# Filler matmuls ahead of lone products in a chunked recurrence, two-block layer on one core

## The chip, the cores and the metric

One core of one Trainium2 chip runs the whole program. The metric is the device time of one execution in microseconds (us); the kernel before has a median of 2063.27 us over 3 runs (2058.55 to 2068.33).

## The reference, cut to what matters

The reference is a stack of two blocks on 512 tokens of width 1024: an RWKV-7 mixer with two attention groups and an output projection, and then a sparse-attention layer, an HGRN2 layer and two gated feed-forward layers. The change lies in the RWKV-7 part alone. It computes, for 8 heads of 64 by 64 state,

```
def step(S, inp):
    r_t, w_t, k_t, v_t, kk_t, a_t = inp
    sa = jnp.einsum('bhvk,bhk->bhv', S, -kk_t)
    S = (S * w_t[:, :, None, :]
         + sa[..., None] * (kk_t * a_t)[:, :, None, :]
         + v_t[..., None] * k_t[:, :, None, :])
    y = jnp.einsum('bhvk,bhk->bhv', S, r_t)
    return S, y
```

over 512 steps. The inputs of the recurrence are prepared elementwise (a decay, a rate `a`, a key normed per head), and a per-head term `sum(r * k * r_k) * v` is added to its output.

## The kernel before, in words

The program is a row of stages, each a block with one instruction stream for each engine, and a barrier of all engines between two stages (`end_stage`, line 87). Weights flow in slabs of 512 KB through a ring of four. Three stages matter here.

**stage_rwkv_prep** (line 494) prepares the recurrence. TensorE makes four head sums of squares (L548), eight products of the two low-rank projections (L555), and, when VectorE has worked through a tile `m` of four (L582 to L591, semaphore `rk_out`), one head sum of `r * k * r_k` into bank `m` (L559). VectorE multiplies the four sums with v at its very end (L595). The order of the work on each engine is that of the code.

**stage_rwkv_chunks** (line 613) computes the recurrence in eight chunks of 64 steps (`NCH` is 8, `CH` is 64). The order is written out by `rwkv_steps` (line 598): ten turns, each with five levels, and at each level the names in `first` belong to chunk `s`, those in `rest` to chunk `s - 1` and those in `state` to chunk `s - 2`. So turn 0 holds the first part of chunk 0 alone, turn 1 the first part of chunk 1 and the `rest` of chunk 0, turns 2 to 7 all three kinds, turn 8 the `rest` of chunk 7 and the `state` of chunk 6, and turn 9 the `state` of chunk 7. TensorE walks this list (the loop `for key in steps`): it waits until the bank of the product is free (`before`), then for the operands (`need`), then issues the product. Products `ga` and `gb` are L701, `ma` and `mb` L706, `vt` L713, `bt` L716, `et` L746, both parts of `uy` L768 and L773, `y` L782, `st` L787 and `yt` L792; all others (`p1`, `p1t`, `p2`, `p2t`, `r2`, `p3t`, `r3`, `r4`, `x`, `xt`, `x2t`, `v1`, `w`, `sa`) go through the helper `each`, eight 64 by 64 matmuls at L688. Six banks go round for all of these but `uy` and `y`, which have banks 6 and 7. ScalarE and VectorE copy or add the results out of the banks in the same order (L806 to L815; L846 to L893), and `p1` also waits for three GpSimd operations (L828, L829, L831), which start when `gb` is out of its bank.

**stage_middle** (line 1024) follows. It loads eight small tables by DMA, and TensorE starts with L1062, L1064 and L1067.

The helper `warm` (line 161) is in the kernel already: it issues `n` matmuls of the identity with 256 columns of constants into a bank that the next product overwrites (L164). Before the change the two attention stages use it.

```
def warm(c, pe, bank, n):
    for _ in range(n):
        pe.matmul(bank[:, 0:2 * P], con(c, "ident"), c.cst[:, 0:2, :], start=True, stop=True)
```

Of the kernel before, what the change touches and what calls it, by code (L numbers as in the profile page):

```python
# [160 lines left out]
# [4 lines that stand above are left out]
# [97 lines left out]
def con(c, name):  # L262
    return c.cst[:, CB[name], :]


def wk(c, at, *shape):

    n = int(np.prod(shape))
    v = c.work[:, at:at + n]
    if len(shape) == 1:  # L270
        return v
    names = "abcd"[:len(shape)]
    return v.rearrange(f"p ({' '.join(names)}) -> p {' '.join(names)}", **dict(zip(names[1:], shape[1:])))
# [205 lines left out]
NCH = T // CH  # L479
# [14 lines left out]
def stage_rwkv_prep(c):  # L494
# [11 lines left out]
    with nc.Block() as block:  # L506

        @block.sync
        def _(sp):
            sp.dma_start(c.reset[:, :], c.a["reset"]).then_inc(reset_in, 16)  # L510
# [33 lines left out]
        @block.tensor  # L544
        def _(pe):
            for m in range(4):
                pe.wait_ge(sq_out, m + 1)
                pe.matmul(c.bank[4 + m][:, :], con(c, "blk"), c.h[:, m, :], start=True, stop=True).then_inc(norm_made, 1)  # L548
            pe.wait_ge(tanh, 1)
            for m in range(4):  # L550
                for j in range(2):
                    if m >= 2:
                        pe.wait_ge(up_out, 2 * (m - 2) + j + 1)
                    rows = slice(HD * j, HD * j + HD)
                    pe.matmul(c.bank[2 * (m % 2) + j][:, :], c.wup[rows, m * P:(m + 1) * P], wa[rows, 0, :],  # L555
                              start=True, stop=True).then_inc(up_made, 1)
            for m in range(4):
                pe.wait_ge(rk_out, m + 1)
                pe.matmul(c.bank[m][:, :], con(c, "blk"), iclr[:, m, :], start=True, stop=True).then_inc(rk_made, 1)  # L559

        @block.vector
        def _(dve):
# [50 lines left out]
def stage_rwkv_chunks(c):  # L613
# [6 lines left out]
    w = [c.h[:, 6 + i, :] for i in range(2)]  # L620
# [7 lines left out]
    yt = wk(c, 8192, 4, T)  # L628
# [3 lines left out]

    by_dve = ("ga", "gb", "ma", "mb", "r2", "r3", "r4", "xt", "v1", "w", "sa", "st", "yt")
    made_at = {key: i + 1 for i, key in enumerate(steps)}
    out_at, turn, before, held = {}, {}, {}, {}
    counts = {"dve": 0, "act": 0}
    for key in steps:
# [16 lines left out]
    def bank(key):  # L654
        return c.bank[turn[key]]

    def need(eng, *key):

        e, n = out_at[key]
        eng.wait_ge(dve_out if e == "dve" else act_out, n)  # L660
# [17 lines left out]
    with nc.Block() as block:  # L678
# [6 lines left out]
        def _(pe):  # L685
# [5 lines left out]
            for key in steps:  # L691
                name, ch = key
                b = buf[ch % 2]
                if before.get(key):
                    need(pe, *before[key])
                if name in ("ga", "gb"):
                    for h in range(4):

# [1633 lines left out]
def program(nc, aps, out):  # L2332

    with ExitStack() as ctx:
        c = Ctx(nc, ctx, aps)
        alloc(c)
        stages = (
            lambda: stage_in(c),
            lambda: stage_rwkv_prep(c),
            lambda: stage_rwkv_chunks(c),  # L2340
            lambda: stage_middle(c),
            lambda: stage_nsa(c),
            lambda: stage_project(c, "out", PLAN["out"], 1.0, ("rms", ("final_g", 0), None, 0), dsa_parts),
            lambda: stage_dsa_in(c),
            lambda: stage_dsa(c),
            lambda: stage_project(c, "wo", PLAN["wo"], ALPHA, ("ln", ("ln_g", 0), ("ln_b2", 0)), ffn_parts),
            lambda: stage_ffn(c, 0),
            lambda: stage_hgrn(c),
            lambda: stage_project(c, "ho", PLAN["ho"], ALPHA, ("ln", ("ln_g", 2 * KT), ("ln_b2", 2 * KT)), ffn_parts, c.big[:, 8:16, :]),
            lambda: stage_ffn(c, 1),  # L2350
            lambda: stage_store(c, out),
        )
        for stage in stages:
            stage()
            c.end_stage()
# [148 lines left out]
```

## Time and profile before

| what | value |
|---|---|
| median of 3 runs | 2063.27 us (2058.55 to 2068.33) |
| the profiled execution, its own time | 2068.71 us |
| its span, first to last instruction | 2066.5 us |
| mean granted TensorE clock | 0.927 |
| TensorE busy | 1865.5 us, 90% of the span |
| VectorE busy | 935.9 us, 45% |
| ScalarE busy | 840.5 us, 41% |
| GpSimd busy | 251.9 us, 12% |
| filler matmuls (L164) before | 324 records for 162 matmuls |
| chunk stage, first product to the next stage's | 260.77 to 428.76 us |

Durations below are of the one profiled execution, with times counted from its span's start. An f32 matmul leaves two records in the trace. PEclk is the TensorE clock that was granted in a stretch, as a share of full speed: 0.50 is 1.2 GHz, 1.00 is 2.4 GHz, and a value between them is a stretch that had some of both. In a timeline row the first number is the start, the second the time covered, xN the number of records, and the bracket the idle time of the engine before it with what ended it; matmuls overlap one another, so a row's cover is longer than the time until the next product can be issued.

### The profile page before, as it was taken

To read this page: it belongs to the slowest core of one execution; us is meant where nothing else is said; L and a number is where in the kernel's file an instruction comes from. 1 tells how busy PE (TensorE), PEld (TensorE's weight loads), DVE (VectorE), ACT (ScalarE), POOL (GpSimd) and SP (SyncE) were. 2 spreads that over 40 slices of the span, in tenths; PEclk is the share of its full clock that TensorE was granted. 3 is DMA by queue.
4 is the path that set the end of the run, shared out by engine and by line. 5 is a ranking of instruction groups with operands and counts; after the bars stand their busy time and mean duration, and the time that the engine had idled before them with its cause. 6 is when DMAs were issued, how large, how long until landed. Compare 5 with 4: busy or idle time off the path is not lost. (4 is left out here: it accounts for less than half of the span.)

```text
span 2066.5 us, 31549 instructions
## 1 busy us (share of the span) xinstructions
PE 1865.5 (90%) x12592; PEld 1512.1 (73%) x12592; DVE 935.9 (45%) x1622; ACT 840.5 (41%) x1359; POOL 251.9 (12%) x209
## 2 busy tenths in 40 slices
PE   5999389969978889988999999979999879999996
PEld 4888188857756657666788888868887768888885
DVE  2343935463355677745333333265554443333333
ACT  4322334434533443543443432275654343434222
POOL 3000223220003220002100000032221020000000
PEclk9999559869989989998999999999999879999998
DMA  4321010010012100002223233222221213233331
GB/s 167 99 92 56 0 43 3 3 45 1 1 42 69 59 23 1 1 27 76 82 91 101 92 101 92 92 79 71 71 78 37 72 51 98 95 98 95 99 95 51
DMA packets 37762, 131.69 MB, mean 64 GB/s; under 512 B 4816, under 2 KB 5136, under 8 KB 37392
## 3 DMA queue, kind: packets, MB, share of 16 engines
q1 hardware_dynamic: 36784, 127.91, 19.8%
q8 instruction: 83, 1.36, 0.3%
q10 hardware_dynamic: 864, 2.17, 0.3%
q14 instruction: 31, 0.25, 0.0%
HBM read 127.17 MB, written 2.10 MB: 63 GB/s over the span
## 5 line engine op out<-in xcount | busy, mean ns | idle before, releaser
L138 DVE TENSOR_TENSOR big_parts<-ring,big_parts 128x1024 fp32r<-128x1024 f32 x164 | 205.0, 1252 | 526.3 <-ACT big_parts L133 526.3
L156 PE MATMUL bank<-h_parts,big_parts 128*128 128x512 f32 x960 | 381.3, 397 | 26.3 <-POOL y_parts L1406 17.6
L157 PE MATMUL bank<-y_parts,big_parts 128*128 128x512 f32 x960 | 377.7, 393 | 0.0
L158 PE MATMUL bank<-h_parts,big_parts 128*128 128x512 f32 x960 | 377.1, 393 | 0.0
L133 ACT ACTIVATE big_parts<-ring 128x1024 fp32r<-128x1024 f32 x164 | 173.7, 1061 | 287.6 <-PE bank L158 287.4
L156 PEld LDWEIGHTS bank<-h_parts,big_parts 128*128 128x128 f32 x960 | 182.8, 190 | 67.5 <-issue 28.6
L158 PEld LDWEIGHTS bank<-h_parts,big_parts 128*128 128x128 f32 x960 | 182.7, 190 | 38.5
L157 PEld LDWEIGHTS bank<-y_parts,big_parts 128*128 128x128 f32 x960 | 182.7, 190 | 37.0
L157 PE MATMUL bank<-y_parts,work_parts 128*128 128x512 f32 x456 | 181.4, 398 | 0.0
L138 DVE TENSOR_TENSOR work_parts<-ring,work_parts 128x1024 fp32r<-128x1024 f32 x65 | 79.3, 1222 | 167.7 <-ACT work_parts L133 167.7
L133 ACT ACTIVATE work_parts<-ring 128x1024 fp32r<-128x1024 f32 x65 | 68.7, 1060 | 206.0 <-PE bank L158 175.9
L156 PE MATMUL bank<-big_parts 128*128 128x512 f32 x352 | 136.9, 389 | 0.0
L157 PE MATMUL bank<-work_parts,big_parts 128*128 128x512 f32 x352 | 136.9, 389 | 0.0
L158 PE MATMUL bank<-big_parts 128*128 128x512 f32 x352 | 136.9, 389 | 0.0
L156 PE MATMUL bank<-h_parts,work_parts 128*128 128x512 f32 x232 | 94.8, 409 | 23.6 <-DVE work_parts L138 19.8
L973 ACT ACTIVATE work<-work 128x256 f32<-128x256 f32 (+4 forms) x128 | 67.1, 524 | 112.7 <-DVE work L995 112.5
L156 PE MATMUL bank<-work_parts 128*128 128x512 f32 (+1 forms) x256 | 97.7, 382 | 5.7 <-POOL y_parts L180 3.8
L157 PEld LDWEIGHTS bank<-y_parts,work_parts 128*128 128x128 f32 x456 | 88.2, 193 | 18.6 <-issue 0.2
L158 PE MATMUL bank<-work_parts 128*128 128x512 f32 (+1 forms) x256 | 97.0, 379 | 0.0
L164 PE MATMUL bank<-cst 128*128 128x256 f32 x324 | 96.5, 401 | 0.0
L158 PE MATMUL bank<-h_parts,work_parts 128*128 128x512 f32 x232 | 92.9, 401 | 0.0
L995 DVE CUSTOM_DVE_ANT_0 work<-bank,big 128x256 f32<-128x256 f32 (+3 forms) x112 | 53.9, 481 | 83.0 <-PE bank L944 72.4
(402 smaller groups left out, 3020.3 us busy)
## 6 DMA issues: line engine op xcount, KB each, us to landing
ring<-in_wstream SPq DMA_DIRECT2D x229, 512.0 KB, 3.5
x<-in_xt SPq DMA_DIRECT2D x4, 512.0 KB, 7.7
out_t<-x SPq DMA_DIRECT2D x8, 256.0 KB, 2.0
work<-in_memt ACTq DMA_DIRECT2D x1, 1024.0 KB, 14.6
work<-in_cw SPq DMA_DIRECT2D x1, 1024.0 KB, 5.1
cst<-in_cst ACTq DMA_DIRECT2D x1, 704.0 KB, 7.7
cos<-in_reset SPq DMA_DIRECT2D x2, 256.0 KB, 2.7
big<-work SPq DMA_DIRECT2D x4, 128.0 KB, 4.2
```

Of the source, the lines that this page charges most:

```text
L133: act.activation(self.parts[:, self.place_of(n), 0, :, :], self.ring[:, n % RING, :, :], ACT.Copy).then_inc(self.slab_cast, 1)
L138: dve.tensor_tensor(self.parts[:, self.place_of(n), 1, :, :], self.ring[:, n % RING, :, :], self.parts[:, self.place_of(n), 0, :, :].bitca ...
L156: pe.matmul(out, w[0], x[0], start=start, stop=False, skip_group_check=True)
L157: pe.matmul(out, w[0], x[1], start=False, stop=False, skip_group_check=True)
L158: return pe.matmul(out, w[1], x[0], start=False, stop=stop, skip_group_check=True)
L164: pe.matmul(bank[:, 0:2 * P], con(c, "ident"), c.cst[:, 0:2, :], start=True, stop=True)
L973: act.activation(e, e, ACT.Exp, bias=self.low[:, n:n + 1], scale=-1.0, accum_out=self.den[:, n:n + 1])\
L995: dve.tensor_tensor_reduce(self.weights(n), self.c.bank[self.SCORES[n % 3]][:, 0:u.keys], u.mask, -self.scale, 3e38, ALU.add, ALU.min, sel ...
```

## The change

It issues fillers at two places. In the preparation stage six go ahead of the wait for each of the four head sums, and three behind the last. In the chunk stage two go ahead of each product named in the set `lone`: nine products of chunk 0 and seven of chunk 7, behind the wait for the bank and ahead of the wait for the operands. With 27 and 32 that makes 59 filler matmuls. Nothing is removed.

```diff
@@ stage_rwkv_prep, tensor
             for m in range(4):
+                warm(c, pe, c.bank[6], 6)
                 pe.wait_ge(rk_out, m + 1)
                 pe.matmul(c.bank[m][:, :], con(c, "blk"), iclr[:, m, :], start=True, stop=True).then_inc(rk_made, 1)
+            warm(c, pe, c.bank[6], 3)
@@ stage_rwkv_chunks
     made_at = {key: i + 1 for i, key in enumerate(steps)}
+    lone = {(n, 0) for n in ("p1", "p2", "p3t", "r4", "et", "x", "x2t", "v1", "w")}
+    lone |= {(n, NCH - 1) for n in ("et", "x", "x2t", "v1", "w", "sa", "yt")}
     out_at, turn, before, held = {}, {}, {}, {}
@@ stage_rwkv_chunks, tensor
                 if before.get(key):
                     need(pe, *before[key])
+                if key in lone:
+                    warm(c, pe, bank(key), 2)
                 if name in ("ga", "gb"):
```

The set is a table, so here is what it does to TensorE's order. The first place is turn 0 of the chunk stage, from the last two transposes to `r4` of chunk 0. Before (L688 rows are `p1`, `p1t`, `p2` and `p2t`):

```order
L713 MATMUL bank4<-cst,big 128x128 x4
L716 MATMUL bank5<-cst,work 128x128 x4
L688 MATMUL bank0<-big 64x64 x8
L688 MATMUL bank1<-big 64x64 x8
L688 MATMUL bank2<-big 64x64 x8
L688 MATMUL bank3<-big 64x64 x8
```

and now (L692 is the same helper, moved down by the new lines; the rows from bank 5 on are `p3t`, `r3` and `r4`):

```order
L719 MATMUL bank4<-cst,big 128x128 x4
L722 MATMUL bank5<-cst,work 128x128 x4
L164 MATMUL bank0<-cst 128x256 x2
L692 MATMUL bank0<-big 64x64 x8
L692 MATMUL bank1<-big 64x64 x8
L164 MATMUL bank2<-cst 128x256 x2
L692 MATMUL bank2<-big 64x64 x8
L692 MATMUL bank3<-big 64x64 x8
L692 MATMUL bank4<-big 64x64 x8
L164 MATMUL bank5<-cst 128x256 x2
L692 MATMUL bank5<-big 64x64 x8
```

Two fillers stand ahead of the first product of each level, in its own bank; the other products of the level follow without any. The second place is the end of the stage: `w` of chunk 7, then `uy`, `sa`, `y` and `yt` of chunk 7. Before:

```order
L688 MATMUL bank0<-big,y 64x64 x8
L768 MATMUL bank7<-work,h 64x64 x16
L773 MATMUL bank7<-work 128x128 x4
L688 MATMUL bank1<-work,h 64x64 x8
L782 MATMUL bank7<-work,h 64x64 x8
L792 MATMUL bank2<-cst,work 128x64 x4
```

and now:

```order
L164 MATMUL bank0<-cst 128x256 x2
L692 MATMUL bank0<-big,y 64x64 x8
L774 MATMUL bank7<-work,h 64x64 x16
L779 MATMUL bank7<-work 128x128 x4
L164 MATMUL bank1<-cst 128x256 x2
L692 MATMUL bank1<-work,h 64x64 x8
L788 MATMUL bank7<-work,h 64x64 x8
L164 MATMUL bank2<-cst 128x256 x2
L798 MATMUL bank2<-cst,work 128x64 x4
```

`uy` and `y`, which are not in the set, get none.

## Rows read from the trace of the kernel before

**Rows 1.** The page: granted clock in 40 slices of the span, in tenths.
```profile
PEclk9999559869989989998999999999999879999998
```
**Rows 2.** Stretches: turns 0, 1, 2 with 3, 4, and turns 8 with 9.
```profile
260.77:277.61 16.84, 12.55 (x184) 11.63 (x186) 3.72 (x8) 4.98 (x12) 3.70 (x3) 0.60 0.34 126
277.61:296.71 19.10, 18.08 (x285) 17.31 (x284) 6.84 (x16) 7.26 (x18) 3.71 (x3) 0.50 0.01 2
296.71:332.15 35.44, 33.98 (x726) 32.06 (x725) 18.20 (x41) 16.66 (x40) 12.11 (x14) 0.85 0.01 3
332.15:349.11 16.96, 15.14 (x371) 14.20 (x368) 9.46 (x22) 8.32 (x20) 6.04 (x7) 1.00 0.01 2
402.57:428.76 26.19, 21.61 (x257) 19.61 (x257) 7.09 (x16) 4.68 (x11) 0.04 (x1) 0.51 0.01 2
```
**Rows 3.** Timeline and stretches: the twelve fillers that open the attention stage.
```profile
469.62 7.94 PE L164 MATMUL bank<-cst 128*128 128x256 f32 x24
477.39 0.27 PE L953 MATMUL bank<-cst,work 128*31 128x128 f32 x1
...
470.00:475.00 5.00, 5.00 (x13) 3.98 (x13) 0.43 (x6) 0.68 (x4) 0.00 (x0) 0.53 0.00 0
475.00:480.00 5.00, 5.00 (x32) 3.81 (x31) 0.71 (x6) 1.43 (x7) 0.00 (x0) 1.00 0.00 0
```
**Rows 4.** Timeline: end of the preparation stage.
```profile
212.23 5.97 PE L555 MATMUL bank<-big,wup 64*128 64x512 f32 x16 [2.63 <-ACT big L520]
...
243.41 2.07 PE L559 MATMUL bank<-work,cst 128*128 128x512 f32 x2 [25.22 <-DVE work L591]
...
257.14 2.08 PE L559 MATMUL bank<-work,cst 128*128 128x512 f32 x2 [2.50 <-DVE work L591]
259.26 0.69 DVE L595 TENSOR_TENSOR y<-bank,big 128x512 f32<-128x512 f32 x1 [0.37 <-PE bank L559]
```
**Rows 5.** Timeline: turn 0 of the chunk stage.
```profile
264.48 1.26 POOL L828 TENSOR_TENSOR big<-h,cst 64x512 f32<-64x512 f32 x1 [23.13 <-DVE h L862]
...
268.28 1.15 PE L688 MATMUL bank<-big 64*64 64x64 f32 x32 [1.88 <-issue]
...
270.71 4.98 PE L688 MATMUL bank<-big 64*64 64x64 f32 x80 [1.28 <-ACT big L806]
271.87 1.62 ACT L806 ACTIVATE big<-bank 64x256 f32<-64x256 f32 x4 [1.30 <-PE bank L688]
...
275.73 0.86 DVE L851 TENSOR_TENSOR big<-bank,big 64x256 f32<-64x256 f32 x2 [1.30 <-PE bank L688]
276.74 1.12 PE L688 MATMUL bank<-big 64*64 64x64 f32 x16 [1.04 <-DVE big L851]
```
**Rows 6.** Timeline: products of turns 4 and 7, at full clock.
```profile
338.84 1.15 PE L688 MATMUL bank<-big 64*64 64x64 f32 x32 [1.18 <-issue]
339.79 0.66 PE L688 MATMUL bank<-big,work 64*64 64x64 f32 x16
...
384.88 1.24 PE L701 MATMUL bank<-work 64*64 64x128 f32 x26
386.84 0.66 PE L713 MATMUL bank<-cst,big 128*128 128x128 f32 x4
387.86 0.51 PE L746 MATMUL bank<-cst,big 64*64 64x64 f32 x10
389.23 1.16 PE L773 MATMUL bank<-work 128*128 128x128 f32 x8
395.92 1.09 PE L782 MATMUL bank<-work,h 64*64 64x64 f32 x16
396.94 1.16 PE L787 MATMUL bank<-work 128*128 128x128 f32 x8
```
**Rows 7.** Timeline: end of the chunk stage, start of the next.
```profile
402.57 0.51 PE L746 MATMUL bank<-cst,y 64*64 64x64 f32 x10 [0.54 <-DVE y L851]
...
427.57 0.43 DVE L893 COPY work<-bank 128x256 f32<-128x256 f32 x1 [3.49 <-PE bank L792]
...
437.08 2.87 DVE L1136 TENSOR_TENSOR work<-big,work 128x496 f32<-128x496 f32 x2 [1.44 <-DMA work<-in_cmask]
```

## The prediction

> **What bounds the kernel now.** I read the page's clock slices first [rows 1]. TensorE is busy for 90% of the span, so its clock is what matters, and the two slices at five tenths are the fifth and sixth of 51.7 us each, 207 to 310 us. That is the end of the preparation stage and turns 0 and 1 of the chunk stage.
>
> The stretches by turn [rows 2] say what this costs. Turn 1 takes 19.10 us at a clock of 0.50 and is busy for 18.08 of them, so it is bound by TensorE at half speed. Turn 4, with a third set of products on top, takes 16.96 at 1.00. Turn 0 takes 16.84 at 0.60, and turns 8 and 9 together 26.19 at 0.51. The reader should see two things: these are the stretches that the change touches, and having work to do did not bring the clock up: 19 us of nearly solid 64 by 64 products in turn 1 ran at half.
>
> Fillers are matmuls of 128 rows and 128 columns. The attention stage has twelve that start at half clock, and the clock goes up while nothing else runs on TensorE: 0.53 over 470 to 475, 1.00 from 475 [rows 3]. 0.53 over 5 us is 0.3 us at full, so it rose at about 474.7, 5.1 us after the first filler.
>
> **Price of a filler.** Those 24 records fill the 7.77 us until the next matmul [rows 3]. With 5.1 us at half and 2.67 at full, and a record at full taking half of one at half (an assumption from the two clock levels), (5.1 + 2 x 2.67) / 24 = 0.435 us a record at half. A filler is two records: 0.87 us at half, 0.435 at full. A pair is 1.74 or 0.87.
>
> **Preparation, 27 fillers.** The first six start when L555 is done, near 218.2, and are over by 221 at full, in a gap of 25.22 us [rows 4]; 22 us of idle time follow, so they bring nothing and cost nothing. The sum of tile 0 starts at 243.41 at half, and six fillers follow at once. A steady run of 128 by 128 work took 5.1 us to lift the clock [rows 3]; here that is by 248.5. Up to then 0.87 us x 6 = 5.2 us of fillers are partly at half, and tile 1, due 4.58 us after tile 0 ((257.14 - 243.41) / 3), starts about 1 us late. Nobody waits: VectorE reads the sums only at its end. From tile 2 on, 2.6 us of fillers fit in the 4.58. VectorE's last multiply starts 2.12 us after the last sum (259.26 against 257.14); at full I take 1.06, so it ends near 258.9 instead of 259.95. The three closing fillers end near 257.14 + 0.9 + 1.3 = 259.3 and now end the stage. Gain 0.5 us. Bounds: -2 if the clock is not up (sum and fillers then end near 257.14 + 1.7 + 2.6 = 261.5), +1.
>
> **Turn 0, 4 pairs.** The first product `p1` waits for GpSimd, whose chain is unchanged. In turn 4, at full clock, the product behind that wait starts 338.84 - 332.15 = 6.7 us after its turn did; in turn 0 it takes 268.28 - 260.77 = 7.5. With nothing of a previous chunk ahead of GpSimd I take 6.4, which gains 1.1. TensorE has issued its own work by then (3.0 us at full: 384.88 to 387.86 [rows 6]), and the pair ahead of `p1` falls in the wait: free. From `p1` on, a level is a product, its copy and the next product. `p2` follows `p1` by 2.43 at full (268.28 to 270.71, [rows 5], where the clock was up for the moment). `p3t` then waits for two copies: 0.7 until the first starts and 1.62 for both, 2.4 in all; `r3` is 0.47 later (two products take 0.95, 338.84 to 339.79 [rows 6]), its VectorE add ends 0.7 + 0.86 after that, and `r4` starts. That is 6.4 + 2.4 + 2.4 + 0.5 + 1.7 = 13.4, and the turn ends 0.5 later: 13.9 against 16.84. The three inner pairs (0.87 each) end before the operands are there: `p1` and `p1t` plus a pair is 1.8 against 2.4; `p2`, `p2t`, `r2` and a pair is 2.3 against 2.4; `p3t`, `r3` and a pair is 1.8 against 2.2. They are free as long as the clock is up; at half, 1.74 each, they would not be. Gain 3.0.
>
> **Turn 1, 5 pairs.** At full, TensorE's part is 3.0 for the products that open it, 14 products of the L688 kind at 0.47 (6.6), and 5 pairs (4.4); nothing hides the last four, since TensorE is the bound here. `p1` of chunk 1 cannot start before 6.4, and `et` with its pair is done at 4.4: 2.0 idle. Sum 16.0 against 19.10. Gain 3.1. Without fillers but at full it would be 12.5 (the wait until 6.4, then 13 products at 0.47), so the cure costs three of the six it could give.
>
> **Turns 2 and 3** get no fillers but may inherit the clock: 35.44 at 0.85 against two times 16.96 [rows 2]. Gain 1.5 at most.
>
> **Turns 8 and 9, 7 pairs.** At full, the products are: eight of the 0.47 kind, 3.8; `uy` twice (389.23 - 387.86 - 0.47 = 0.9 for the first part, 1.06 for the second, by `st`'s), 3.9; `y` twice at 1.02, 2.0; `st` 1.1; `yt` twice at 0.4, 0.8 [rows 6]. That is 11.6, and pairs 6.1: 17.7. On top 1.6 us of waits that remain: for the last `sa` copy (1.2) and short ones. So the last copy ends 19.3 after the first product, where it was 428.00 - 402.57 = 25.4 [rows 7]. Gain 6.1.
>
> **What does not follow.** The next stage starts sooner by the whole gain and with a clock that is up. But its VectorE chain waits for a DMA that is issued at the stage's start, until 437.08 [rows 7], and TensorE's head start ends there. I count nothing.
>
> Sum with the clock up throughout: 0.5 + 3.0 + 3.1 + 1.5 + 6.1 = 14.2 us.
>
> **Relapses.** The waits for GpSimd in turns 0 and 1 leave 2.6 and 2.0 us idle (6.4 less 3.0 and a pair; 6.4 less 4.4). In turn 0 before, the clock that was up at 268.28 was at half again for the products from 270.71 on, after idle gaps of 1.88 and 1.28 [rows 5], so it can fall there. A relapse puts `p1`, `p1t` and the next pair at half: 0.95 + 0.87 more, of which turn 0 has 0.6 to spare (2.4 - 1.8), and in turn 1 `x` and `xt` also (0.95): 1.2 to 2.8 us. I count one of 2.2. Forecast: 14.2 - 2.2 = 12.0.
>
> The Trainium skill ("TensorE: Matmul & The Clock Gate", Part 1) says that sustained TensorE activity opens the clock and idle time closes it, whatever the matmuls are. By that rule turn 1 before should have run at full; the trace disagrees (18.08 of 19.10 busy, 0.50). By the rule, turn 1 would have nothing to gain, and the sum would be 5.4 in place of 12.0; I go by the rows, and keep that outcome as the second rival.
>
> The profiled execution took 2068.71 us, 5.4 more than the median, so the sum reads 2056.7 on it and **2051.3 on the median**. A measurement here can tell about 0.5%, 10.3 us, from no change, so the forecast lies only just beyond that.
>
> **Rivals.**
> - *The clock relapses at each wait.* For it: the two gaps above. 14.2 less 1.2 and 2.8, and 2.2 for one more in turn 8, leaves 8: 2055.3. Chance 0.27.
> - *The other executions had less to win.* The median execution is 5.4 us faster than the profiled one, and part of that may be a turn 1 with its clock up. Then turn 1 loses 3.5 to its fillers (16.0 against 12.5) where I count a gain of 3.1: 12.0 - 6.6 = 5.4, or 2057.9. One trace of one execution can't exclude it. Chance 0.14. (By the skill's rule this would be the ordinary case.)
> - *No relapse at all*: 2049.1, chance 0.12.
> - *Slower: the fillers do not lift the clock.* They come in pairs between 64 by 64 products, not in twelves, and 19 us of solid work did not lift it. Then 16 pairs cost 27.8; idle time in turns 0, 1, 8 and 9 takes up at most 4.29 + 1.02 + 4.58 = 9.9 [rows 2]. In the preparation a sum and six fillers take 6.95 in place of 4.58, three times: 7.1, and the closing three 1.8. Together 26.8: 2090. Against: twelve in a row did lift it. It decides once pairs at half outweigh what they speed up. Chance 0.05.
> - *The change does not do what it says*: the first six fillers are that already, and harmless. If those of the preparation all fail and the chunk stage starts at half, its own pairs must do it, and 3 to 4 us of the gain are lost; this is in the range.
>
> **How the numbers follow.** Forecast 0.42, the rest as above. Faster by over 0.5% is the forecast, most of it, and the no-relapse case: 0.53. Within it are the second and third, and the edge of the forecast: 0.42. Slower 0.05. The range runs from 2043 (no relapse, all bounds good, and 6 us for the spread that three runs of before show) to 2062 (the third case with 4 us of spread); it leaves out the slower case and the tails.
>
> **What would show it.** L164 with 442 records. Granted clock 1.00 in the preparation from 249 on, in turn 8 and 9, and mostly in turns 0 and 1. Turn 0 at 14 us, turn 1 at 16 to 18, turns 8 and 9 at 19 to 21. The wait for the DMA in the next stage longer, not shorter. It is wrong if turn 1 stays at 0.50 with the fillers in it, or if the chunk stage shrinks by its 14 us and the total doesn't.

## The result, and the profile after

The changed kernel is slower: 2075.32 us at the median of 20 executions (2066.72 to 2088.34) against 2067.03 us for before (20 executions, 2056.41 to 2069.69). The ratio is 1.0054, 95% interval 1.004 to 1.0068. The forecast was 2051.3, and its range ended at 2062; a slower kernel had a chance of 0.05. The spread between executions grew from 13 to 22 us, which is a result too. The profiled execution took 2084.95 us with a span of 2082.8, so it is one of the slower ones; further below is a second profile of the same kernel, of an execution of 2075.29 us, which is the median of these 20.

The page of after, TensorE's busy share and the granted clock in 40 slices, which answer to [rows 1]:

```profile
PE   5999499997978899989899999979999879999996
...
PEclk9999886777989999999999999999999879999998
L164 PE MATMUL bank<-cst 128*128 128x256 f32 x442 | 131.4, 410 | 0.0
```

All 59 fillers ran (442 records against 324). The two slices at five tenths became two at eight. The four after them read 9, 8, 6 and 9 before and 6, 7, 7 and 7 now. The stretches of the chunk stage by turn, turns 0 to 7 and then 8 with 9 from `et` on, answer to [rows 2]:

```profile
259.25:278.87 19.62, 17.30 (x201) 13.94 (x202) 3.63 (x8) 4.97 (x12) 3.70 (x3) 0.66 0.30 109
278.87:297.51 18.64, 18.64 (x304) 15.88 (x304) 7.09 (x16) 7.25 (x18) 3.71 (x3) 0.80 0.01 2
297.51:314.09 16.58, 14.30 (x362) 13.49 (x360) 8.55 (x20) 8.31 (x20) 6.04 (x7) 0.98 0.01 3
314.09:340.77 26.68, 26.68 (x369) 25.31 (x368) 9.79 (x22) 8.43 (x20) 6.03 (x7) 0.50 0.01 2
340.77:359.60 18.83, 18.19 (x369) 17.08 (x369) 9.27 (x21) 8.44 (x20) 6.03 (x7) 0.82 0.01 2
359.60:381.50 21.90, 20.73 (x371) 19.68 (x368) 9.93 (x23) 8.31 (x20) 6.03 (x7) 0.69 0.01 3
381.50:400.40 18.90, 18.26 (x369) 17.15 (x367) 9.24 (x21) 8.43 (x20) 6.02 (x7) 0.81 0.01 2
400.40:424.40 24.00, 22.83 (x376) 20.84 (x371) 11.09 (x25) 8.31 (x20) 8.37 (x11) 0.68 0.01 2
424.40:446.13 21.73, 19.54 (x282) 16.14 (x281) 6.45 (x14) 4.68 (x11) 0.04 (x1) 0.89 0.01 2
```

Read the clock, third number from the end. Turn 3 ran wholly at half and took 26.68 us, where turn 4 of before at full took 16.96 [rows 2]. A turn at half thus costs 9.7 us more. Turns 2 to 7 hold no filler (but for one pair at the very end of the last stretch but one), and that is where the time went. Turn 0, with the change's pairs, is 2.8 us longer than before. Its timeline on TensorE answers to [rows 5]:

```profile
262.16 1.03 PE L164 MATMUL bank<-cst 128*128 128x256 f32 x4
265.50 1.85 PE L692 MATMUL bank<-big 64*64 64x64 f32 x32 [2.31 <-POOL big L837]
267.29 2.07 PE L164 MATMUL bank<-cst 128*128 128x256 f32 x4
269.29 2.83 PE L692 MATMUL bank<-big 64*64 64x64 f32 x48
272.05 2.07 PE L164 MATMUL bank<-cst 128*128 128x256 f32 x4
```

The pair ahead of `p1` takes 1.03 us, then 2.31 us of idle time follow, and from there on pairs take 2.07: the clock fell to half at the end of the wait, and at half the pairs fill every gap and more, since no idle time is left in front of the products.

### The profile page after: what moved, and what is told of

The parts are those of the page before. It is cut to its first block and busy times, and to the rows that moved or that the text cites. A ratio compares the mean times of both kernels' runs of the same rounds, so it can differ in the third digit from the quotient of the medians.

```text
span 2082.8 us, 31776 instructions
## 1 busy us (share of the span) xinstructions
PE 1898.5 (91%) x12710; PEld 1539.9 (74%) x12710; DVE 937.1 (45%) x1622; ACT 840.3 (40%) x1359; POOL 251.6 (12%) x209
## 5 line engine op out<-in xcount | busy, mean ns | idle before, releaser
L164 PE MATMUL bank<-cst 128*128 128x256 f32 x442 | 131.4, 410 | 0.0
L164 PEld LDWEIGHTS bank<-cst 128*128 128x128 f32 x442 | 85.5, 204 | 30.2 <-issue 14.7
L158 PE MATMUL bank<-work_parts 128*128 128x512 f32 (+1 forms) x256 | 96.9, 378 | 0.0
```

What stands on the lines that cost most here:

```text
L158: return pe.matmul(out, w[1], x[0], start=False, stop=stop, skip_group_check=True)
```

## The experiments

For before and the two profiles of the change I give the times of turns 0 and 1, turns 2 to 6, and turns 7 to 9 until the next stage's first product, from the stretches by turn.

| kernel | profiled | 0, 1 | 2 to 6 | 7 to 9 |
|---|---|---|---|---|
| before | 2068.71 | 35.9 | 88.2 | 43.9 |
| the change | 2084.95 | 38.3 | 102.9 | 45.7 |
| the change, second profile | 2075.29 | 31.2 | 96.9 | 48.5 |

The rest of the program behind the chunk stage is 1637.7, 1636.6 and 1636.1 us in these three. The first product of the stage starts up to 1.5 us earlier than before; all else is in this stage.

### The parts of the change by themselves

`e1_prep` keeps the preparation's fillers alone:

```diff
-    lone = {(n, 0) for n in ("p1", "p2", "p3t", "r4", "et", "x", "x2t", "v1", "w")}
-    lone |= {(n, NCH - 1) for n in ("et", "x", "x2t", "v1", "w", "sa", "yt")}
+    lone = set()
```

> The 27 fillers of the preparation alone, none in the chunk stage. Where the change lost its time: turns 3 to 7, which hold no filler, took 26.7, 18.8, 21.9, 18.9 and 22.0 us in the profile after, against 17.8, 17.0, 17.4, 18.4 and 16.9 before, all at a clock that had fallen back to half. Theory A (the loss is in those turns: a clock that is raised early falls back in the waits for GpSimd and then stays down through turns of 64 by 64 products): the clock is up at the start of turn 0, falls in it, and the total is within 5 us of before, either way. Theory B (the loss is what the fillers themselves take at half clock, in the chunk stage): 0 to 1 us faster than before.

Measured: 2067.81 us (12 executions), before 2066.41 beside it, ratio 1.0008 (0.9992 to 1.0024): no difference. The clock was up from 250 to 267, through the start of turn 0, and fell in its wait for GpSimd. As expected by A; B's up to 1 us faster is inside the interval too, so this run alone decides nothing. The profiled execution is the slowest of its twelve (2079.34).

`e2_chunk0` keeps the nine pairs of chunk 0 alone (both `warm` lines of the preparation and the second `lone` line taken out):

> The nine pairs of chunk 0 alone. Theory A: most of the loss is here, 6 to 12 us slower than before, and the profile shows turns 3 to 7 at half clock for 10 us or more in all beyond the 10 us of before, in some executions. Theory B: turns 0 and 1 longer by the pairs at half, 4 to 8 us together, turns 3 to 7 as before.

Measured: 2082.36 us (6 executions), ratio 1.0088 (1.0065 to 1.0112), 16 us above before at the median, worse than the whole change and beyond A's 6 to 12. Both theories have a part: turns 0 and 1 took 40.4 us (15.20 and 25.22) against 35.9, and turns 2 to 6 took 96.9 against 88.2.

`e3_chunk7` keeps the seven pairs of chunk 7 alone:

> The seven pairs of chunk 7 alone. In the profile after, turns 8 and 9 with their fillers took 3.1 us less than before. Theory A: 3 us faster than before, or up to 6 if turn 8 starts at full clock. Theory B: 0 to 3 us slower, since the pairs start at half clock.

Measured: 2062.61 us (12 executions), ratio 0.9991 (0.9976 to 1.0006), and 3.8 us below before at the median; the interval includes no difference. In its profile turns 3 to 7 were at full, and so were 8 and 9. Its stretches of turn 6 and of turns 7 to 9, and the first product of turn 8 and of the next stage:

```profile
364.06:381.02 16.96, 15.15 (x372) 14.21 (x369) 9.46 (x22) 8.32 (x20) 6.03 (x7) 1.00 0.01 3
381.02:419.43 38.41, 34.42 (x655) 30.01 (x651) 17.30 (x39) 12.99 (x31) 8.40 (x12) 1.00 0.01 3
...
399.15 0.51 PE L750 MATMUL bank<-cst,y 64*64 64x64 f32 x10
...
419.43 3.67 PE L1066 MATMUL bank<-work,cst 128*128 128x512 f32 x8 [1.23 <-PEq L90]
```

From the first product of turn 8 to the next stage it is 20.28 us, against 26.19 before. The first of the seven pairs stands ahead of that product, in what is counted as turn 7 here, so the fair comparison is that of turns 7 to 9: 38.4 against 43.9, 5.5 us less. In this profile the waits of 1.2 us ahead of `p1` in turns 3 to 7 held no filler, and the clock did not fall in any of them.

`e8_rest0` keeps only the five pairs that stand in turn 1:

```diff
+    lone = {(n, 0) for n in ("et", "x", "x2t", "v1", "w")}
```

> The five pairs of turn 1 alone (et, x, x2t, v1 and w of chunk 0). With all nine pairs of chunk 0 and no others turn 1 took 25.2 us with 17.6 at half, against 19.1 before. If these five pairs are the loss (they start at half clock in a turn that TensorE bounds, 1.74 us each): turn 1 at 23 to 26 us, and 5 to 10 us slower than before. If the pairs of turn 0 are: within 3 us of before.

Measured: 2081.29 us (6 executions), ratio 1.0068 (1.0045 to 1.0091). That is 14 us above before at the median, beyond the 5 to 10 that I expected, and not where I expected it. Turns 1, 2, 3, 4 and 5 of its profile:

```profile
276.93:295.38 18.45, 18.27 (x306) 15.79 (x305) 7.09 (x16) 7.26 (x18) 3.71 (x3) 0.84 0.01 2
295.38:316.96 21.58, 19.70 (x362) 18.78 (x360) 8.69 (x20) 8.33 (x20) 6.05 (x7) 0.69 0.01 3
316.96:335.81 18.85, 18.21 (x370) 17.10 (x369) 9.26 (x21) 8.44 (x20) 6.04 (x7) 0.82 0.01 3
335.81:357.71 21.90, 20.73 (x371) 19.68 (x368) 9.96 (x23) 8.33 (x20) 6.04 (x7) 0.69 0.01 2
357.71:376.65 18.94, 18.30 (x369) 17.19 (x368) 9.25 (x21) 8.44 (x20) 6.04 (x7) 0.81 0.01 3
```

The turn with the pairs (the first line) is 0.65 us shorter than before. The turns behind it alternate between 21.6 to 21.9 and 18.9 us, where at full they take 17.0. Such a couple costs 4.8 + 1.9 = 6.7 us, and this profile has three of the long ones.

### The wait for GpSimd

So most of the loss is in turns without fillers. In the clock's record of all profiles, the falls gather at two places of a turn. One is 8.0 to 9.7 us after its first product; the clock then mostly comes back only 4 to 7 us into the next turn. The other is around its end, 16 us in or later or within 1.2 us of the next turn's start. Those of turns 2 to 6 are mostly short (3 to 7 us), but two lasted 34 us and two 14; those at the end of turn 7 mostly last into turns 8 and 9. The first profile of the change had one of 34 us, which put the whole of turn 3 at half. The first place is behind the wait for GpSimd, which in a turn at full leaves 1.18 us idle ahead of the `p1` product [rows 6]. `e4_all_p1` is the change with a pair in that wait in every turn:

```diff
+    lone |= {("p1", n) for n in range(1, NCH)}
```

> The whole change and a pair ahead of p1 of chunks 1 to 7 also, in the wait for GpSimd (1.18 us idle in the full-clock turns of before). Theory A: the clock no longer falls, or comes back within a turn; turns 3 to 7 near 17 us each, 12 us or more faster than before. Theory B: seven more pairs at 0.9 to 1.7 us each make it 5 to 10 us slower than the change.

Measured: 2061.97 us (12 executions, 2056.41 to 2069.64) beside 2066.41 for before; ratio 0.9989 (0.9974 to 1.0003). Against before it is 4.4 us faster where the change was 8.3 slower (and 4.1 slower in a second measurement, below): seven more pairs took 9 to 13 us off it, and the spread went from 22 to 13 us. Theory B expected 5 to 10 us more. Turns 0, 3 and 4 of its profile:

```profile
259.19:278.71 19.52, 17.20 (x201) 13.84 (x202) 3.62 (x8) 4.98 (x12) 3.71 (x3) 0.67 0.30 109
...
313.36:333.05 19.69, 19.05 (x376) 17.68 (x372) 9.56 (x22) 8.45 (x20) 6.02 (x7) 0.83 0.01 2
333.05:349.97 16.92, 16.02 (x375) 14.79 (x372) 9.45 (x22) 8.33 (x20) 6.04 (x7) 1.00 0.01 3
```

Turn 4 is as long as without the pair (16.92 against 16.96): in this wait a pair at full clock is free. The median is short of A's "12 us or more faster than before"; turn 0 still loses its 2.7.

`e5_p1_only` has a pair ahead of every `p1` and nothing else; `e6_p1_chunk7` has those and chunk 7's:

> A pair ahead of p1 of all eight chunks, nothing else: eight pairs, all in the wait for GpSimd. So far: the profile with a pair ahead of every p1 and the whole change had turns 4 to 9 at full clock. Theory A (the clock falls in those waits, and a pair there holds it up): turns 0 and 1 as before, turns 2 to 7 with less than 5 us at half in all, 3 to 6 us faster than before. Theory B (what counts is what the fillers of chunk 7 bring at the end): no faster than before, turns 8 and 9 at half as before.

> Pairs ahead of every p1 and the seven of chunk 7; the other eight of chunk 0 and the preparation's left out. Theory A: turns 0 and 1 as before (36 us), 3 to 7 at 17, turns 8 and 9 at 21: 6 to 9 us faster than before, the fastest so far. Theory B: as fast as the kernel with chunk 7's pairs alone, 4 us faster than before at the median.

Measured: 2070.53 us, ratio 1.0014 (0.9994 to 1.0035), and 2060.94 us, ratio 0.9987 (0.9965 to 1.0009). The first is a miss for A, which expected 3 to 6 us faster; its total, and turns 8 and 9 at half, are what B expected. Its executions fall into groups near 2061, 2070.5 and 2080. In its profile turns 2 to 5 were as A says (16.9 to 17.5), but it lost the clock 16.4 us into turn 5 and again 17.6 us into turn 7, at the ends of turns, and then ran the last turns at half. So the pairs did what A says in their own place, and the time went in falls at the ends of turns instead. The second kernel had 6 of 11 executions between 2057.5 and 2061, and four above 2070; the profiled one (2076.78) had the clock at half all through turns 1 and 2, 20.2 and 26.7 us. A pair ahead of `p1` in turn 1 at half costs 1.1 us (20.2 against 19.10) and does not lift the clock by itself. Neither kernel can be told from before, and the second is 6.2 us below it at the median where chunk 7's pairs alone are 3.8, with intervals that overlap: a pair in each of these waits has a clear effect only on top of the change.

`e11_p1_small` is the change, with pairs of 64 by 64 in the same place:

```diff
+                if name == "p1" and ch:
+                    for _ in range(2):
+                        pe.matmul(bank(key)[0:HD, 0:2 * P], con(c, "ident")[0:HD, 0:HD], c.cst[0:HD, 0:2, :], start=True, stop=True)
```

> The change and, ahead of p1 of chunks 1 to 7, a pair of 64 by 64 matmuls of 256 columns in place of the 128 by 128 ones that took 13 us off the change: the same time on TensorE, a quarter of the array. Theory A (it is the work in the wait that keeps the clock): turns 3 to 7 at half as often as with the change, 2070 to 2080. Theory B (any pair there shifts the products out of a bad place): as good as the 128 by 128 pairs, 2062.

> The change itself, again, beside the other three and for a second profile. Theory A: turns 3 to 7 longer than 17 us at a clock that has fallen to half, by 10 us or more in all, though perhaps not the same turns as in the first profile; median 2070 to 2080 with a spread of 15 us or more between executions, where before has 13. If the first profile was a rare one: turns 3 to 7 near 17 each and the loss elsewhere.

Measured side by side: small pairs 2070.65 us (ratio 1.002, 1.0005 to 1.0035), the change again 2071.04 (ratio 1.0031, 1.0009 to 1.0052; 2062.57 to 2087.30), before 2066.97. Small pairs bring nothing, where the large ones had brought 9 us at least, so it is the large matmuls in the wait and not the shift in time. The large pairs were measured at another time, with before 0.6 us faster; against their own before the two intervals (0.9974 to 1.0003 with large pairs, 1.0005 to 1.0035 with small) do not overlap. Turns 0, 1 and 2 of the change's second profile:

```profile
260.32:274.30 13.98, 11.44 (x201) 9.49 (x202) 3.63 (x8) 4.98 (x12) 3.70 (x3) 1.00 0.43 151
274.30:291.53 17.23, 15.46 (x307) 13.10 (x304) 7.00 (x16) 7.25 (x18) 3.71 (x3) 1.00 0.01 3
291.53:312.60 21.07, 19.19 (x362) 18.27 (x360) 8.70 (x20) 8.31 (x20) 6.05 (x7) 0.71 0.01 3
```

Here the clock lasted through turns 0 and 1, which is what I had forecast, and it fell in turn 2, behind a wait of 1.88 us. A wait does not always do that: turn 1 had 1.77 us idle ahead of its `p1`, and the clock stayed up. These are the rows of turn 1 behind that wait:

```profile
280.60 1.15 PE L692 MATMUL bank<-big 64*64 64x64 f32 x32 [1.77 <-issue]
281.67 1.13 PE L164 MATMUL bank<-cst 128*128 128x256 f32 x4
282.74 1.15 PE L692 MATMUL bank<-big 64*64 64x64 f32 x32
```

The four stretches around the fall in turn 2 show it, busy share and clock together: idle time in the second, half clock in the third.

```profile
289.00:294.00 5.00, 5.00 (x105) 4.48 (x106) 3.90 (x9) 0.00 (x0) 0.00 (x1) 1.00 0.01 3
294.00:299.00 5.00, 3.12 (x95) 2.85 (x94) 0.58 (x2) 2.88 (x7) 4.93 (x6) 1.00 0.02 3
299.00:304.00 5.00, 5.00 (x115) 5.00 (x111) 2.53 (x6) 3.45 (x10) 1.12 (x2) 0.64 0.01 3
304.00:309.00 5.00, 5.00 (x51) 4.66 (x51) 0.69 (x1) 1.58 (x4) 0.00 (x0) 0.50 0.00 0
```

Counted over all profiles, turns 2 to 7: 13 falls 8.0 to 9.7 us into a turn in the nine without full-size pairs ahead of `p1` (54 turns; none of them in before's own or in that of `e3_chunk7`), and 1 in the eight that have them (48 turns). The clock was up 7.9 us into 52 and 45 of these turns. There is one profile for each kernel, two for the change.

### What kind of matmul lifts the clock

`e7_prep64` gives the preparation its 27 fillers as 64 by 64 matmuls:

```diff
+                for _ in range(6):
+                    pe.matmul(c.bank[6][0:HD, 0:2 * P], con(c, "ident")[0:HD, 0:HD], c.cst[0:HD, 0:2, :], start=True, stop=True)
```

> The 27 fillers of the preparation as 64 by 64 matmuls of the same 256 columns, none in the chunk stage. If it is being busy that raises the clock: 1.00 by 249, as with the 128 by 128 ones, which had it at 1.00 from 250 on. If the size of the matmul counts: 0.50 up to the first product of turn 0, with sums delayed by 2.4 us a tile, and the stage's end 3 to 8 us later than with those.

One execution, 2083.57 us; two stretches and two rows of its timeline:

```profile
246.00:251.00 5.00, 5.00 (x11) 2.33 (x11) 4.90 (x9) 0.00 (x0) 0.00 (x0) 0.50 0.00 0
...
266.00:271.00 5.00, 5.00 (x10) 1.69 (x8) 0.69 (x1) 0.00 (x0) 0.00 (x0) 0.50 0.00 0
...
246.71 5.38 PE L559 MATMUL bank<-cst 64*64 64x256 f32 x12
252.02 2.07 PE L561 MATMUL bank<-work,cst 128*128 128x512 f32 x2
```

TensorE was busy without a gap from 246 to 271 and stayed at 0.50; all of this was 64 by 64 matmuls but for three head sums of 2.07 us each and the end of a fourth. With the 128 by 128 fillers in the same places the same stretch reads, in the profile of after:

```profile
246.00:259.00 13.00, 11.02 (x43) 7.60 (x41) 12.15 (x23) 0.00 (x0) 0.00 (x0) 1.00 0.00 0
```

The stage began its first chunk product at 272.3 instead of 259.25, 13.0 us later where I expected 3 to 8: three groups delayed it and the closing three fillers did too.

### Filling the waits

`e9_wait7` is `e4_all_p1` with seven fillers ahead of `p1` of chunk 0, where 2.31 us were idle; `e10_wait7_bare1` also leaves out the five pairs of turn 1:

```diff
-                    warm(c, pe, bank(key), 2)
+                    warm(c, pe, bank(key), 7 if key == ("p1", 0) else 2)
```

> The change, a pair ahead of p1 of chunks 1 to 7, and seven fillers in place of two ahead of p1 of chunk 0, where the profile after had 2.31 us of idle time behind the pair and then the clock at half. Theory A (an idle wait lets the clock fall, and a filled one does not): turn 0 stays at full and takes the 14 us that I had predicted for it, turn 1 16 to 18, turns 2 to 7 at 17, so 14 us or more faster than before, near 2051. Theory B (fillers only shift the products against whatever sets the clock): turn 0 no shorter than the 19.5 us of the kernel with two fillers there, and the total that kernel's, 2062.

> As the one with seven fillers, but without the five pairs of turn 1 (et, x, x2t, v1, w of chunk 0). Theory A: if the clock is up through turn 0, it stays up in turn 1 through its own products and the pair ahead of p1, and the turn takes 13 to 15 us instead of 16: 3 us faster than with them. If it falls, turn 1 takes 19 to 20 and the median is 2 to 4 us slower than with them.

Measured: 2063.06 us (ratio 0.9992, 0.9967 to 1.0016; 2053.42 to 2079.94) and 2057.79 us (ratio 0.9973, 0.9958 to 0.9989; 2054.72 to 2070.11). Turn 0 was at full in both, 13.99 and 14.00 us. The first missed its 2051: only two of twelve executions were below 2055, and its profile lost the clock near the end of turn 3, 16.6 us in. The second is the first that is clearly faster than before, although its clock fell in turn 1, behind 1.53 us of idle time (17.87 us for the turn). For that case I had expected it to be 2 to 4 us slower than the first; its median is 5.3 faster, with intervals that overlap.

`e13_p1_5` puts five fillers there, `e14_p1_5_r4` adds one ahead of `r4` of chunks 1 to 7, and `e15_r4_noprep` is that without the preparation's:

```diff
+                    warm(c, pe, bank(key), 1 if name == "r4" and ch else {("p1", 0): 7, ("p1", 1): 5}.get(key, 2))
```

> As the kernel without the five pairs of turn 1, but five fillers in place of two ahead of p1 of chunk 1, where its clock fell after 1.53 us of idle time. Theory A (a fall some 8 us into a turn comes from the idle wait for GpSimd): turns 0 and 1 at full, 14 and 14 to 15 us, and 3 us off its 2057.8. Theory B: turn 1 falls elsewhere, no gain.

> The same, and one filler ahead of r4 of chunks 1 to 7, in a wait for VectorE of 0.43 us. In the profiles so far the falls that pairs ahead of p1 left over come 16 to 19 us into a turn or in the first us of the next, behind these waits, and mostly last 3 us. Theory A: fewer of them, a median of 2052 to 2055 and a narrower spread. Theory B: 7 x 0.3 us slower than without, spread the same.

> The same as the last without the 27 fillers of the preparation. The clock is then at half at the start of turn 0, and the seven fillers ahead of p1 (6.1 us at half in a wait of some 2 us) hold up turn 0. Theory A: turn 0 at 17 to 20 instead of 14, 3 to 6 us slower than with them.

Measured, before at 2066.36:

| kernel | median (executions, spread) | ratio to before |
|---|---|---|
| e13 | 2053.94 us (6; 2049.51 to 2056.22) | 0.9938 (0.9924 to 0.9951) |
| e14 | 2052.66 us (6; 2051.53 to 2053.66) | 0.9936 (0.9924 to 0.9949) |
| e15 | 2059.82 us (7; 2058.12 to 2060.63) | 0.9968 (0.9957 to 0.9979) |

Turns 0, 1, 3, and 7 to 9 of e14:

```profile
261.67:275.66 13.99, 13.59 (x210) 11.39 (x212) 3.63 (x8) 4.98 (x12) 3.72 (x3) 1.00 0.41 151
275.66:290.35 14.69, 13.54 (x299) 11.91 (x297) 6.74 (x16) 7.14 (x18) 3.72 (x3) 1.00 0.02 4
...
306.69:323.62 16.93, 16.58 (x378) 15.07 (x375) 9.46 (x22) 8.33 (x20) 6.04 (x7) 1.00 0.02 4
...
374.40:413.31 38.91, 36.38 (x661) 31.05 (x658) 17.32 (x39) 13.00 (x31) 8.41 (x12) 0.97 0.01 3
```

The stage takes 151.6 us, 16.4 less than before. `e13_p1_5` is 12.4 us below before where `e10_wait7_bare1` was 9.2, the 3 us that A expected, and its profile has turn 1 at full in 14.67 us. The filler ahead of `r4` makes no measurable difference to the median (1.3 us between two sets of six); the narrower spread, 2 against 7 us, agrees with A but rests on six executions each. Without the preparation's fillers turn 0 took 16.40 us, less than the 17 to 20 expected: it was at half for its first 5.7 us and then, with the seven fillers in the wait, at full to its end, where in before the clock came up at the same place for 3.4 us only. The total is 7.2 us above that of e14, more than A's 3 to 6. The clock fell 8.7 us into turn 2 in spite of the pair there, the one fall of that kind among the kernels with pairs.

## Why the prediction was wrong, point by point

- **The sign** was wrong: 12.0 us faster was forecast, 8.3 us slower at the median was measured.
- **Price of a filler** was too low by 10 to 23%. The time from a pair to the product behind it is 0.96 us at full behind 128 by 128 products and 1.07 between 64 by 64 ones (281.67 to 282.74 above), where I had 0.87, and 2.00 at half (267.29 to 269.29), where I had 1.74.
- **Preparation**, forecast 0.5 us: 3.24 us from the last sum to the first chunk product, against 3.63 before: 0.4. The clock was up as forecast.
- **Turn 0 at full**, forecast 13.9: 13.98 in the second profile, but 19.62 in the first, where the clock fell, so it was luck of the execution whether this came out. **Turn 1 at full** with its pairs, 16.0: 17.23. Without pairs, 12.5: 14.69 with five fillers ahead of `p1`. So the five pairs cost 2.5 there, not 3.5, but both times were 1.2 to 2.2 too low. With the pairs it is the price above (four pairs, 0.8 us) and products at 0.5 in place of 0.47; without them it is waits at four levels behind `p1`, 1.5 us in the profile of `e13_p1_5`, that I had left out.
- **Turns 8 and 9 at full**: the last copy was to end 19.3 us after the first filler, the next stage to begin near 20.1. In `e3_chunk7` it is 21.3 (398.09 to 419.43), and over turns 7 to 9 the gain is 5.5 of the 6.1.
- **Next stage**, nothing: it was right. Its wait for the DMA grew from 1.44 to 2.78 us (in the profile of after), and what follows the chunk stage took 1635.7 to 1637.8 us in all profiles but one (1640.2).
- **The step that failed is "Relapses"**: "I count one of 2.2". I looked for falls only in turns 0 and 1 (in a rival also in turn 8) and took turns 2 to 7 as either unchanged or better ("Gain 1.5 at most"). The row for it was before me: 1.18 us idle in the same wait in a full-clock turn [rows 6], so each turn could fall. Also the price was wrong. I priced one level at half; but a fall mostly lasts until 4 to 7 us into the next turn, so it costs 6.7 us (21.9 + 18.9 against 2 x 17.0), or 9.7 and more when a turn stays down. The one relapse that I did count, in turn 0, cost 5.6 us there (19.62 against 13.98) and 1.4 in turn 1 (18.64 against 17.23), not 2.2. The rival that relapses at each wait (2055.3) had the mechanism in part and the same two errors. The slower rival had another mechanism: fillers do lift the clock.
- **What the runs showed in its place.** The change raises the clock ahead of turn 2, and then the clock falls in turns that hold no filler: turns 2 to 6 took 102.9 and 96.9 us in its two profiles, against 88.2. Pairs of turn 1 alone make the kernel 14 us slower at the median though their own turn gets shorter; filling the wait in each turn brings 9 to 13 us. That ties the falls 8 to 10 us into a turn to the idle wait. In the first profile they cost 6.8 us in turns 5 and 6 and 5.9 in turn 7 (24.0 against 18.1 in `e3_chunk7`). The largest loss, 11.6 us in turns 3 and 4, came from a fall at the end of turn 2, and no run shows what brings those about.
- **What stays open** is why before, with the same waits, keeps its clock better: it rises by itself in turn 2, and the one profile has two short falls at the ends of turns 2 and 5 and none at 8 us. The place in the turn where the clock rises seems to decide whether it falls in a later wait, but the kernel with the preparation's fillers alone also rose in turn 2, and fell in turns 5 and 7. That was not tested by itself. Which executions of one kernel fall is open too.

## What to carry to other kernels

Look at the whole loop before you raise a clock at its start. In this kernel a raised clock was lost again in waits of the loop's body that held nothing, and a fall was paid for until well into the next turn: 6.7 us and more, several times the idle time ahead of it. What worked here was to fill the waits to their length with full-size matmuls (seven fillers instead of two where 2.31 us were idle, five instead of two where 1.53 were) and to leave alone products that have no wait ahead of them. A pair in each wait and nothing else did not pay. Where the clock decides, one profile is a sample: look at the spread of the executions, and take the price of a fall from a whole turn at half.

## What the runs showed of the hardware that I had not expected

A busy TensorE is not enough to have the clock up; the size of the matmuls made the difference here. 25 us without a gap, nearly all 64 by 64 work but for three sums of 2.07 us, stayed at 0.50 in the one execution of `e7_prep64`, where 128 by 128 fillers in the same places had 1.00 from 246 on. Small pairs in a wait did nothing (2070.65 against 2071.04 us), where 128 by 128 ones of the same length took 9 us or more off. The Trainium skill ("TensorE: Matmul & The Clock Gate", Part 1) has the clock follow how busy TensorE is; these runs disagree with it where the matmuls are small. And falls can repeat in step with the program: three times in a row every second turn of `e8_rest0` took 21.6 to 21.9 us and the one between 18.9.
